# Pooling layer: the groups in the order of widths 2, 8, 16, 4, and the low part of the pooled columns on VectorE

## The reference

```python
POOL_WINDOWS = (2, 4, 8, 16)          # one per group of 512 columns

def causal_pool_minus_self(u, window):
    c = jnp.cumsum(u32, axis=1)
    c_shift = jnp.pad(c, ((0, 0), (window, 0), (0, 0)))[:, :S]
    mean = (c - c_shift) / jnp.minimum(jnp.arange(S) + 1, window)[None, :, None]
    return mean - u32

def pooling_mixer(u, w_in, w_group, scale, w_out):
    xb, z = jnp.split(u @ w_in, 2, axis=-1)             # 2048 columns each
    xg = xb.reshape(B, S, 4, 512)
    pooled = jnp.stack([causal_pool_minus_self(xg[:, :, gi], w)
                        for gi, w in enumerate(POOL_WINDOWS)], axis=2)
    mixed = jnp.einsum('bsgi,gio->bsgo', pooled, w_group).reshape(B, S, 2048)
    return (mixed * scale * jax.nn.silu(z)) @ w_out
```

## Time and profile before

| what | us |
|---|---|
| median of three runs | 994.96 |
| lowest and highest of them | 992.82, 998.03 |
| the profiled execution | 992.32 |
| its span | 990.5 |
| first unit of the pooling layer starts, in the span | 582.4 |
| last unit of its output product ends | about 754.6 |

### The profile page before, as it was taken

How to read it: one execution, slowest core, us unless ns; L and a number is a source line. 1 busy time by engine, 2 the same in 40 slices (tenths; PEclk the granted TensorE clock), 3 DMA queues, 4 the chain that set the end, 5 groups by cost and what they waited for, 6 DMA issues and landing times.

```text
span 990.5 us, 16827 instructions
## 1 busy us (share of the span) xinstructions
PE 925.2 (93%) x6793; PEld 867.7 (88%) x6793; DVE 640.2 (65%) x1006; ACT 500.1 (50%) x700; POOL 313.5 (32%) x270
## 2 busy tenths in 40 slices
PE   5999999988878997989999999899999999999988
PEld 5999987668667986769999999899999998988987
DVE  5776665896574788864677666678556544655642
ACT  5534455454574676674443353434535336575632
POOL 6433322342013225122443336965203000223320
PEclk9999999998999998999999999899999999999998
DMA  9886444344014425316386444253663752424401
GB/s 248 207 208 192 159 170 170 107 149 170 31 58 144 168 66 186 115 41 170 110 231 191 170 171 155 101 204 136 255 218 126 246 185 86 167 89 171 170 1 43
DMA packets 123170, 148.20 MB, mean 150 GB/s; under 512 B 9521, under 2 KB 79070, under 8 KB 123102
## 3 DMA queue, kind: packets, MB, share of 16 engines
q1 hardware_dynamic: 122384, 146.16, 45.6%
q0 software_dynamic: 464, 1.02, 0.4%
q10 hardware_dynamic: 254, 0.07, 0.0%
HBM read 146.18 MB, written 1.05 MB: 149 GB/s over the span
## 4 chain that ended last, share of the span: by engine, by line
PE 60%; DVE 8%; ACT 7%; POOL 3%; issue 2%; DVEq 0%; ACTq 0%; POOLq 0%
PE acc L1618 43%; PE aux L1618 16%; DVE wlo L862 2%; ACT whi L464 1%; POOL arena L1473 1%; ACT work L657 1%; ACT arena L490 1%; POOL arena L1474 1%; POOL arena L1472 1%; ACT whi L456 1%; ACT work L664 1%; ACT work L655 1%; DVE score L1110 1%; DVE arena L969 1%; DVE top L1109 1%
## 5 line engine op out<-in xcount | busy, mean ns | idle before, releaser
L862 DVE TENSOR_TENSOR wlo<-raw,whi 128x2048 fp32r<-128x2048 f32 (+5 forms) x118 | 281.3, 2410 | 104.2 <-ACT whi L456 102.5
L1618 PE MATMUL acc<-xh,whi 128*128 128x256 f32 x1128 | 323.7, 287 | 7.7 <-DVE wlo L862 4.2
L1618 PE MATMUL acc<-xl,whi 128*128 128x256 f32 x1128 | 320.9, 285 | 0.0
L1618 PE MATMUL acc<-xh,wlo 128*128 128x256 f32 x1128 | 320.8, 284 | 0.0
L456 ACT ACTIVATE whi<-raw 128x2048 fp32r<-128x2048 f32 (+5 forms) x118 | 202.9, 1748 | 86.5 <-PE aux L1618 45.3
L1618 PEld LDWEIGHTS acc<-xh,whi 128*128 128x128 f32 x1128 | 218.0, 193 | 9.9 <-issue 5.8
L1618 PEld LDWEIGHTS acc<-xl,whi 128*128 128x128 f32 x1128 | 218.1, 193 | 0.0
L1618 PEld LDWEIGHTS acc<-xh,wlo 128*128 128x128 f32 x1128 | 217.8, 193 | 0.0
L1618 PE MATMUL acc<-whi,xh 128*128 128x512 f32 (+1 forms) x208 | 82.6, 397 | 7.9 <-DVE arena L969 4.0
L1537 POOL CAST yh<-ytmp 128x256 fp32r<-128x256 f32 x24 | 16.9, 705 | 217.4 <-DVE ytmp L1393 123.3
L1618 PE MATMUL aux<-yh,whi 128*128 128x256 f32 x288 | 81.9, 284 | 0.0
(11 more groups left out here) (331 smaller groups left out, 1757.2 us busy)
## 6 DMA issues: line engine op xcount, KB each, us to landing
raw<-in_a_w_in SPq DMA_DIRECT2D x52, 512.0 KB, 6.7
raw<-in_sb_w_in SPq DMA_DIRECT2D x48, 512.0 KB, 5.6
raw<-in_b_w_in SPq DMA_DIRECT2D x36, 512.0 KB, 5.4
raw<-in_pool_w_in SPq DMA_DIRECT2D x32, 512.0 KB, 5.7
raw<-in_a_w_out SPq DMA_DIRECT2D x16, 512.0 KB, 4.9
raw<-in_pool_w_out SPq DMA_DIRECT2D x16, 512.0 KB, 5.1
raw<-in_sb_w_out SPq DMA_DIRECT2D x16, 512.0 KB, 5.0
raw<-in_a_w_in SPq DMA_DIRECT2D x16, 256.0 KB, 5.6
```

The costliest lines, as they stand in the source:

```text
L862: TT(wlo[b][:, lo:hi], (raw_third if third else raw[b])[:, lo:hi], whi[b][:, lo:hi].bitcast(F32), ALU.subtract).then_inc(lo_ready, 1)
L1618: return nc.tensor.matmul(out_, lhsT, rhs, start=start, stop=stop, skip_group_check=True)
```

## The change

The order becomes (0, 2, 3, 1), widths 2, 8, 16, 4. The low part `pl` is made by VectorE, as the last step of its z branch, and GpSimd waits for it before it starts the next place.

```diff
-        ORDER = (2, 3, 1, 0)
+        ORDER = (0, 2, 3, 1)
         POOL_UNITS = [("x", 0), ("z", 0), ("x", 1), ("mix", 0), ("z", 1), ("x", 2), ("mix", 1), ("z", 2), ("x", 3),
                       ("mix", 2), ("z", 3), ("mix", 3)]
...
                     for c in range(2):
                         ins = TT(arena[:, 39 + 2 * c:41 + 2 * c, :], psum[c], rb, ALU.mult)
                     ins.then_inc(sem("z_raw"), 1)
+                    dve.wait_ge(sem("ph_ready"), g + 1)
+                    TT(pl[:, :, :], pad[2][:, :, mid], ph[:, :, :].bitcast(F32), ALU.subtract).then_inc(sem("pl_ready"), 1)
...
                 pool.wait_ge(sem("xb_taken"), 2 * g + 2)
+                if g:
+                    pool.wait_ge(sem("pl_ready"), g)
...
                 TT(pad[2][:, :, mid], pad[src][:, :, mid], pad[0][:, :, mid], ALU.subtract).then_inc(sem("pooled"), 1)
-                pool.wait_ge(sem("ph_ready"), g + 1)
-                TT(pl[:, :, :], pad[2][:, :, mid], ph[:, :, :].bitcast(F32), ALU.subtract).then_inc(sem("pl_ready"), 1)
-                pool.wait_ge(sem("pl_ready"), g + 1)
```

## The result

| | us |
|---|---|
| before, median of 8 runs | 994.68 (990.84 to 998.03) |
| changed, median of 8 runs | 1004.46 (999.34 to 1006.86) |
| ratio, 95% interval | 1.0092 (1.0068 to 1.0116) |
| profiled execution, before and changed | 992.32 and 1004.75 |
| its span, before and changed | 990.5 and 1003.0 |

The change costs 9.8 us between the medians, 6.8 to 11.5 by the interval of the ratio. The forecast was 1004.8, with +9.8 worked out as a sum of terms. The sum was not right in every term. In the two profiled executions the stretch from the end of x1 to the end of mix3 took 89.7 us before (618.92 to 708.60) and 102.4 us in the changed kernel (616.78 to 719.14), 12.7 us more. The spans differ by 12.5, but that is not the layer alone: the changed execution came to the end of x1 2.1 us earlier and took 2.0 us more from mix3's end to the end of the span.

A forecast was written before the change was run, and what follows sets the result against it. TensorE, busy 925.2 of 990.5 us, was taken to bound the kernel. The terms -2.5 - 0.7 + 1.2 + 9.5 + 2.3 gave +9.8, on the median of 994.96 a forecast of 1004.8 us, range 999.5 to 1010.

The forecast's parts named there:

- gap before mix0: Place 0: TensorE's wait before mix0 falls from 4.89 to 2.4 us, a gain of 2.5.
- slow clock behind it: Time lost to TensorE's lower clock after a gap: 1.6 us behind mix0's gap, 2.3 behind mix3's.
- gap before x3: Place 2: a new wait of 1.2 us before x3, whose low half waits for GpSimd's division; bounds 0 and 2.4.
- gap before z3: Before z3: no wait forecast, 0 us.
- gap before mix3: Place 3: a gap of 10.4 us, a loss of 9.5, as the low part stands behind the first output unit's split.
- The bound of 11 for a late load: Place 3: upper bound of 11 us on the loss of 9.5 before mix3; the lower was 8.5.
- the one on places 1 and 2: Places 1 and 2: an x unit hides the low part before mix1 and mix2; only x3 waits, 1.2 us.
- The argument on place 3: Place 3: the load issued after z3's split keeps its lead on z3's end within half a microsecond; loss 9.5 us.
- Rival 1: Before mix1 and mix2: VectorE and GpSimd obstruct each other there too, making both late; +14.5 us, 1009.5; chance 0.09.
- Rival 2: Place 3: mix3 finds the low part ready and is not late; -2.9 us, 992, at best 989.3; chance 0.05.
- The rule beside it: Whole kernel: VectorE over GpSimd, about twice as slow with two inputs, for elementwise work; makes the move a pure gain.
- Rival 3: Place 0: silu holds up the high part and mix0 starts no earlier than 623.8; +13.0 us, 1008; chance 0.06.

The follow-up runs named there:

- e10: e3 with the widths back in the order of before (8, 16, 4, 2); ratio 0.9970 (0.9937 to 1.0002) against before.
- e1: Kernel before with only the order changed to widths 2, 8, 16, 4, low part still on GpSimd; ratio 1.0011 (0.9988 to 1.0035).
- e4: e3 with VectorE taking z0 from PSUM before it splits mix0's weights at place 0; ratio 0.9928 (0.9900 to 0.9956) against before.
- e2: Changed kernel with the order as before (8, 16, 4, 2), so only the low part moved to VectorE; ratio 1.0113 (1.0083 to 1.0142) against before.
- e3: Changed kernel with place 3's low part made earlier, ahead of VectorE's wait for z3; ratio 0.9964 (0.9940 to 0.9988) against before.
- e5: Changed kernel with the first output unit's weight split put behind the low part at place 3; profiled only, gap before mix3 3.82 us.
- e6: Changed kernel with only two of GpSimd's four additions at place 2, half that window sum left out; profiled only, gap before mix3 10.30 us.
- e9: Changed kernel without any edit, a second profiled execution; no ratio, 102.3 us from the end of x1 to the end of mix3.
- e8: Changed kernel with widths 2, 8, 4, 16, the two last places swapped; profiled only, gap before mix3 14.24 us.

## Why the prediction was right, point by point

| term | forecast | measured |
|---|---|---|
| gap before mix0 (4.89 before) | 2.4 | 2.02 |
| slow clock behind it (2.3 before) | 1.6 | 1.5 |
| gap before x3 | 1.2 | 1.21 |
| gap before z3 | 0 | 2.00 |
| slow clock behind it | 0 | 1.5 |
| gap before mix3 (0.87 before) | 10.4 | 10.29 |
| slow clock behind it | 2.3 | 2.15 |

The clock's terms are the chain's rows less the same number of matmuls at full clock: 30.52 for 240 against 29.0 (e10's 29.05 and the earlier trace rows), 13.24 for 96 against 11.74 (e1's z3, at 690.86), 8.13 for 48 against 5.98 (e4's 5.98 for mix3). The measured terms sum to 20.7 us, against 8.1 before: +12.6, and the layer took 12.7 us more.

**mix3.** Right in mechanism and size. e2 shows that the move alone brings it, e3 that the place in the queue is its cause, e5 which instructions of the queue it consists of. The bound of 11 for a late load wasn't needed.

**mix0.** Right in mechanism: VectorE's splits and not GpSimd set the z take, and the high part waits behind the silu. Changed kernel, ScalarE and VectorE at place 0, beside the earlier trace rows:

```profile
614.13 1.28 DVE L1336 TENSOR_TENSOR arena<-acc,r 128x512 f32<-128x512 f32 x2
...
615.44 1.06 ACT L793 ACTIVATE arena<-arena 128x1024 f32<-128x1024 f32 x1 [6.76 <-DVE arena L1336]
616.40 1.04 ACT L802 ACTIVATE ph<-pad 128x1024 fp32r<-128x1024 f32 x1
...
617.47 1.23 DVE L1339 TENSOR_TENSOR pl<-pad,ph 128x1024 fp32r<-128x1024 f32 x1 [2.07 <-ACT ph L802]
```

Of the 0.4 us by which the gap is shorter, 0.3 stand ahead of the z take: it started 2.65 us before the end of x1 (616.78), and the forecast had 2.3 (616.6 against 618.92). From there to mix0 it took 4.67 us, where the forecast had 4.75.

**x3.** Right in mechanism, and e6 confirms the cause. GpSimd's division at place 2:

```profile
663.25 2.42 POOL L1604 TENSOR_TENSOR pad<-pad,count 128x1024 f32<-128x1024 f32 x1
```

x3's first half came at 663.35, waited for it and ended at 667.82. It came only 0.10 us behind the start of the division. Had it come first, it would have ended, at its 2.2 us by itself, at about 665.6, before TensorE wanted it at 666.76. So the term hung on a tenth of a microsecond, and that it agrees to a hundredth is luck.

**z3: missed.** The step that failed is the one on places 1 and 2, which has no wait before z3. It followed the late first half of x3 and stopped there. The second half is late too (it ends at 672.2), and z3's load is issued only behind it, 4.3 us behind the start of x3. That alone makes no gap, as e1 and e3 show. With a load of 7.6 us z3's own split then meets GpSimd's additions. This cost 3.5 us in the profile, gap and clock together. What made the load that slow is open. The argument on place 3 had even used the distance from z3's split to z3's end, for the next unit only.

**The median.** The forecast added the sum to the median. The profiled execution of before lies 2.4 us under its median, that of the changed kernel 0.3 above, and e9, the second profile of the changed kernel, has the same gaps and took 102.3 us for the same stretch; so 12.7 by the traces and 9.8 between medians stand beside each other. By the ratio's interval, 6.8 to 11.5 us, 12.7 is more than the typical run pays, and my 9.8 agrees with what it pays partly because the missed term is not in it. That the time came out within 0.4 us of the forecast is therefore in part luck. Whether z3's gap is absent in some of the timed runs, as in e3, isn't shown.

**Rivals.** Rival 1 (mix1 and mix2 late) fell: the low part of place 1 ended at 645.0, 4 us ahead of mix1, where I had counted 1 to 2, and that of place 2 at 678.2, 1.4 ahead of mix2. With width 16 at place 1 (e2, e10) nothing was to spare: mix1 waited 0.18 and 0.33 us. But its notion that the two engines get in each other's way at one more place was true, at z3. Rival 2 (mix3 in time) fell. The rule beside it, VectorE rather than GpSimd for elementwise work (the Trainium skill, GPSIMD Engine Reference, section "4.1 Engine selection"), holds for the duration: 1.21 us against 2.36. For the time of the kernel it does not hold in the change. With the last low part made early it seems to: e3 has 0.9964 and e1, with the same order and the low part on GpSimd, 1.0011, though their intervals touch; in the old order e10's 0.9970 isn't clear of 1. Rival 3 fell.

## What to carry to other kernels

Before moving a step to a faster engine, write down what stands ahead of it in that engine's queue and what each of those things waits for: here 1.2 us of work, which mix3 waits for, went behind a split that can't start before z3, the unit just ahead of mix3, is done, and cost 10 us. Look at the irregular place of a loop by itself; three places of four had a unit in between that hid the wait. Where an instruction is late, follow it through its second half and the load issued behind it, not only to the first unit that it feeds. And try both halves of a change alone and together: here one wait came only with both.

## What the runs showed of the hardware

The same gap can be followed by a slow clock or not. e8 has the gap of 2.02 us before mix0 (624.59 to 626.61) as the changed kernel has, but 45 matmuls in the next 5.4 us at a clock of 1.00, where the changed kernel has 33 at 0.68 (busy time by stretch of e8):

```profile
626.60:632.00 5.40, 5.39 (x45) 5.40 (x46) 5.40 (x4) 2.25 (x2) 4.14 (x2) 1.00 0.49 181
```

Of the seven profiles with this gap, six have the slow clock behind it; e8 has the same program up to there. The gap of 2.72 us that left the clock at 1.00 in the kernel before stands in the changed kernel too, far behind the pooling layer: 2.71 us, up to 965.17, and then 28 matmuls in 4.9 us at a clock of 0.66. So about 1.5 us can come and go with the same gap at the same place.

Nor does the loss follow the length of the gap. Behind 10.3 us it was 2.15 in the changed kernel and 1.3 in e6 (7.32 us for 48 matmuls against 5.98), behind 14.24 us in e8 2.1 (8.05), and behind 3.82 us in e5 1.5 (7.46).

And the turns of VectorE and GpSimd make small delays jump: a load that took 1.2 us more (7.6 in the changed kernel, 6.4 in e3) moved z3 by 2.0 us.
